# The first gate round in halves of 32 first keys, the second half among V blocks 0 to 31, with ScalarE making eight of 16 tokens' second-key one-hots

## What is computed

```python
q = (h @ w_q).reshape(b, s, 8, 2, 128)               # 8 heads, two half queries
scores = einsum('bshpd,hpnd->bshpn', q, sub_keys)    # 128 scores per half
top_s, top_i = top_k(scores, 16)                     # first keys and second keys
cand = top_s[..., 0, :, None] + top_s[..., 1, None, :]
best_s, best_pos = top_k(cand, 16)                   # expert = first key * 128 + second key
gates = softmax(best_s)
act = gelu(x . u_tab[expert])                        # 8 heads x 16 experts per token
out = sum(gates * act * v_tab[expert])
x = layer_norm(alpha * h + out)
```

## Time and profile before

| | |
|---|---|
| median of 3 executions | 1513.28 us (1513.22, 1513.28, 1518.79) |
| profiled execution, its own time | 1518.35 us |
| its span | 1516.2 us |
| busy share of the span | PE 89%, PEld 63%, DVE 77%, ACT 21%, POOL 44% |
| moved by DMA | 444.24 MB, mean 293 GB/s |
| longest rows of the chain that ended last | PE L1232 34%, DMA of `peer_v` rows 11%, PE L1249 7%, PE L1285 6% |

### The profile page before, as it was taken

The page is one execution under the profiler, slowest core; times in us unless marked ns, Lnnn a source line. Parts: engine busy times, 40 slices in busy tenths (PEclk is TensorE's granted clock), DMA queues, the critical chain, the costliest instruction groups (busy, mean ns, idle before and its releaser), DMA issues.

```text
span 1516.2 us, 18422 instructions
## 1 busy us (share of the span) xinstructions
PE 1354.7 (89%) x6418; PEld 953.7 (63%) x6418; DVE 1175.1 (77%) x2515; ACT 317.7 (21%) x609; POOL 660.3 (44%) x548
## 2 busy tenths in 40 slices
PE   8999989999999996764899799999799999999940
PEld 6787755688888885554444345588688874444410
DVE  5746345778888898779987799989888887666698
ACT  4223010111111011110010355556531110000010
POOL 2244111141443345600365465645365665656572
PEclk9999999999999997875899999999899999999975
DMA  6311422475888989920599999989799999999995
GB/s 230 144 57 56 152 74 96 138 225 174 328 336 342 357 303 401 407 109 1 187 413 415 413 373 364 406 337 391 259 380 383 414 414 412 414 413 415 412 358 215
DMA packets 118283, 444.24 MB, mean 293 GB/s; under 512 B 11568, under 2 KB 24368, under 8 KB 101808
## 3 DMA queue, kind: packets, MB, share of 16 engines
q0 software_dynamic: 73728, 268.47, 46.1%
q1 hardware_dynamic: 43888, 173.56, 29.6%
q10 hardware_dynamic: 576, 1.05, 0.2%
HBM read 440.93 MB, written 2.10 MB: 292 GB/s over the span
## 4 chain that ended last, share of the span: by engine, by line
PE 54%; DVE 17%; DMA 15%; issue 5%; POOL 5%; DVEq 3%; ACT 1%; ACTq 0%; SPq 0%
PE ps L1232 34%; DMA big<-in_peer_v_dram,idx 11%; PE ps L1249 7%; PE ps L1285 6%; DMA big<-in_peer_u_dram,idx 4%; DVE y L1071 3%; POOL big L566 3%; DVE big L1050 2%; POOL big L556 2%; PE ps L1457 2%; DVE pool_mem L1134 1%; DVE ohi L1091 1%; DVE wr L1090 1%; PE ps L1391 1%; PE ps L1372 1%
## 5 line engine op out<-in xcount | busy, mean ns | idle before, releaser
L556 POOL DMA_INDIRECT big<-in_peer_u_dram,idx x256 | 310.1, 1211 | 580.3 <-DVE dots L1050 463.5
L1071 DVE SCALAR_TENSOR_TENSOR y<-big,wgt,y 128x1024 f32<-128x1024 f32 x256 | 328.2, 1282 | 44.4 <-DMA big<-in_peer_v_dram,idx 32.3
L1050 DVE CUSTOM_DVE_ANT_0 big<-big,xh 128x1024 f32<-128x1024 f32 x256 | 311.5, 1223 | 63.1 <-DMA big<-in_peer_u_dram,idx 35.8
L566 POOL DMA_INDIRECT big<-in_peer_v_dram,idx x256 | 289.2, 1130 | 113.8 <-issue 70.2
L1232 PE MATMUL ps<-xT,big 128*128 128x256 f32 x1024 | 230.8, 384 | 11.7 <-issue 11.7
L1285 PE MATMUL ps<-big,pool_mem 128*128 128x512 f32 x512 | 226.1, 597 | 0.0
L1232 PEld LDWEIGHTS ps<-xT,big 128*128 128x128 f32 x1024 | 196.5, 193 | 40.8 <-issue 14.5
L1285 PEld LDWEIGHTS ps<-big,pool_mem 128*128 128x128 f32 x512 | 97.4, 192 | 119.7 <-issue 119.7
L1285 PE MATMUL ps<-y,pool_mem 128*128 128x512 f32 x256 | 116.5, 606 | 0.8 <-DVEq L1207 0.8
L1232 PE MATMUL ps<-xT 128*128 128x256 f32 x512 | 116.0, 386 | 0.0
L1232 PE MATMUL ps<-xT,y 128*128 128x256 f32 x512 | 114.7, 383 | 0.0
(11 more groups left out here) (224 smaller groups left out, 1445.9 us busy)
## 6 DMA issues: line engine op xcount, KB each, us to landing
big<-u_pairs_dram SPq DMA_DIRECT2D x32, 1024.0 KB
big<-v_pairs_dram SPq DMA_DIRECT2D x32, 1024.0 KB
y<-u_pairs_dram SPq DMA_DIRECT2D x16, 1024.0 KB
xT<-u_pairs_dram SPq DMA_DIRECT2D x16, 1024.0 KB
y<-v_pairs_dram SPq DMA_DIRECT2D x16, 1024.0 KB
xT<-v_pairs_dram SPq DMA_DIRECT2D x16, 1024.0 KB
big<-in_w_in_dram SPq DMA_DIRECT2D x24, 512.0 KB, 5.7
pool_mem<-in_peer_w_q_dram SPq DMA_DIRECT2D x12, 1024.0 KB
```

Of the source, the lines that this page charges most:

```text
L556: nc.gpsimd.indirect_dma_start(urow[n % RING], None, peer_u2, bass.IndirectOffsetOnAxis(ap=idx[:, u, e:e + 1], axis=0)).then_inc(s_u[n % R ...
L566: nc.gpsimd.indirect_dma_start(vrow[n % RING], None, peer_v2, bass.IndirectOffsetOnAxis(ap=idx[:, u, e:e + 1], axis=0)).then_inc(s_v[n % R ...
L1050: V.tensor_tensor_reduce(out=urow[n % RING], in0=urow[n % RING], in1=xh[:, u // PH * D:(u // PH + 1) * D], scale=1.0, scalar=0.0, op0=ALU. ...
L1071: V.scalar_tensor_tensor(acc_rows[t], vrow[n % RING], wgt[:, u % 2, e:e + 1], acc_rows[t], ALU.mult, ALU.add).then_inc(s_vadd, 1)
```

## The change

The gate round of 32 groups goes. In its place are 16 teams (0, 0, m) at row 80, of 16 tokens and first keys 0 to 31, and 16 teams (0, 1, m), of first keys 32 to 63, at rows 81 to 109 of DVE. For teams (0, 0, m) DVE makes both `ohj` matrices, in three buffers that take turns (`ohj3`: the two of `ohj` and the memory of `ohl`); for teams (0, 1, m) ACT makes the second one, as in round 1. PE has the teams (0, 1, m) ahead of `expert` 1, 2, 4, 6, 8, 9, 11, ..., 27 of round 0. `dense_weights` now covers 32 keys of 16 tokens; that of team (0, 1, m) follows the DVE work of team m + 2, the last two stand at row 110. `expert` 0 waits for the first 32 keys, `expert` 32 for the others. ACT's gelu of unit 5 moves from ahead of the round to behind team (0, 1, 8).

```diff
-SPREAD = ((1, 0), (1, 1))
+SPREAD = ((0, 1), (1, 0), (1, 1))
...
     def gate_round():
-        for n in range(GROUPS):
-            add("gate", n, by="dve")
+        for m in range(TEAMS):
+            add("team", 0, 0, m, by="dve")
...
         if r == 0:
-            jobs.append(("onehot", (0, 0), None))
+            jobs.append(("onehot", (0, 1, 0), None))
         for n in range(HALF):
+            if r == 0 and n < QUARTER:
+                for m in range(TEAMS):
+                    if n == 1 + m * 7 // 4:
+                        add("team", 0, 1, m, by="dve")
+                        jobs.append(("onehot", (0, 1, m + 1) if m + 1 < TEAMS else (1, 0, 0), None))
+                        if m == 8:
+                            jobs.append(("gelu", (5,), None))
...
-    dense_second_half(0, range(4, 6))
+    dense_second_half(0, range(4, 5))
...
                 if kind == "onehot":
-                    s, m = arg
+                    m = arg[2]
+                    b, n = BANK[TEAM[TEAM0[arg[0:2]] + m - 1]]
+                    act.wait_ge(full[b], n + 1)
...
-                V.tensor_tensor(ohj[:, g % 2], spread(1, 2 * m, NK), both(grid[:], NK), ALU.is_equal)
-                fence().then_inc(s_oh, 1)
+                if g >= TEAMS:
+                    V.tensor_tensor(ohj[:, g % 2], spread(1, 2 * m, NK), both(grid[:], NK), ALU.is_equal)
+                    fence().then_inc(s_oh, 1)
+                for side in range(2) if g < TEAMS else ():
+                    e = 2 * g + side
+                    if e >= 3 and e % 2:
+                        dve.wait_ge(s_ohd, (e - 3) // 2 + 1)
+                    elif e >= 3:
+                        b, used_ = BANK[TEAM[(e - 3) // 2]]
+                        dve.wait_ge(full[b], used_ + 1)
+                    V.tensor_tensor(ohj3[e % 3], spread(1, 2 * m + side, NK), both(grid[:], NK), ALU.is_equal)
+                    fence().then_inc(s_oh, 1)
...
-                x3 = X[:, :, 8 * n:8 * n + 8]
-                V.scalar_tensor_tensor(x3, ps[:, b, :].rearrange("p (t i) -> p i t", t=8), 1.0 / GATE_SCALE, x3,
+                x3 = X[:, QUARTER * s:QUARTER * (s + 1), 16 * m:16 * m + 16]
+                V.scalar_tensor_tensor(x3, ps[:, b, :].rearrange("p (t i) -> p i t", t=16), 1.0 / GATE_SCALE, x3,
                                        ALU.mult, ALU.mult).then_inc(free[b], 1)
...
-                    for g in range(GROUPS):
-                        gate_rows(g)
-                        if g:
-                            dense_weights(g - 1)
-                    dense_weights(GROUPS - 1)
+                    for m in range(TEAMS):
+                        team_rows_of(0, 0, m)
+                        if m:
+                            dense_weights(0, m - 1)
+                    dense_weights(0, TEAMS - 1)
                     fence().then_inc(s_wgtd, 1)
                 for r, s, m in teams_after(n):
                     team_rows_of(r, s, m)
+                    if r == 0 and m >= 2:
+                        dense_weights(1, m - 2)
+                if n == team_rows(0, 1)[-1] + 1:
+                    dense_weights(1, TEAMS - 2)
+                    dense_weights(1, TEAMS - 1)
+                    fence().then_inc(s_wgtd, 1)
...
-                    if i == 0 and r == 0:
-                        pe.wait_ge(s_wgtd, 1)
+                    if i % QUARTER == 0 and r == 0:
+                        pe.wait_ge(s_wgtd, i // QUARTER + 1)
...
-                elif kind == "gate":
-                    n_ = arg[0]
-                    pe.wait_ge(s_oh, n_ + 1)
...
+                        e = 2 * g + t // 8
+                        if g < TEAMS:
+                            hot = ohj3[e % 3]
...
+                        if t == 7 and g < TEAMS:
+                            last.then_inc(s_ohd, 1)
```

More of the change, by code:

```diff
@@ L22 @@
 ROWS = GUNITS * TOPK
-GROUPS = DENSE // 8
 LAG = 2 * TOPK
@@ L177, in dense_first_half @@
                 if n + 1 < TEAMS:
-                    jobs.append(("onehot", (1, n + 1), None))
+                    jobs.append(("onehot", (1, 1, n + 1), None))
             add("act", r, n, by="act" if r == 0 else "dve")
@@ L200, in dense_second_half @@
                 add("team", 1, 0, m, by="act")
-                jobs.append(("onehot", divmod(m + 1, TEAMS), None))
+                jobs.append(("onehot", (1,) + divmod(m + 1, TEAMS), None))
                 if m in between:
@@ L252, in layer @@
     BANK = {(kind,) + arg: (b, n) for kind, arg, _, b, n in JOBS}
-    TEAM = [("team",) + rs + (m,) for rs in SPREAD for m in range(TEAMS)]
-    TEAM0 = {rs: k * TEAMS for k, rs in enumerate(SPREAD)}
+    TEAM = [("team",) + rs + (m,) for rs in ((0, 0),) + SPREAD for m in range(TEAMS)]
+    TEAM0 = {rs: k * TEAMS for k, rs in enumerate(((0, 0),) + SPREAD)}
     ctx = ExitStack()
@@ L334, in layer @@
         ohj = wr[:, :].bitcast(f16).rearrange("p (b q n t) -> p b q n t", b=2, q=2, t=4)
+        ohj3 = [ohj[:, 0], ohj[:, 1]]
         lookd = wr[:, :].bitcast(bf16)
@@ L370, in layer @@
         sel = sb("sel", [P, 2, 2, PH, TOPK])
-        ohl = sel[:].rearrange("p a b h k -> p (a b h k)").bitcast(f16).rearrange("p (q n t) -> p q n t", q=2, t=4)
+        ohj3.append(sel[:].rearrange("p a b h k -> p (a b h k)").bitcast(f16).rearrange(
+            "p (q n t) -> p q n t", q=2, t=4))
+        ohl = ohj3[2]
         gated = sb("gated", [P, 2 * PH, TOPK])
@@ L416, in layer @@
         s_gates, s_selT = sem("gates_ready"), sem("selT_ready")
-        s_oh, s_ohl = sem("onehots_ready"), sem("last_eight_onehots_ready")
+        s_oh, s_ohd, s_ohl = sem("onehots_ready"), sem("first_onehots_used"), sem("last_eight_onehots_ready")
         s_act, s_wgtd = sem("dense_gelu_ready"), sem("dense_weights_ready")
@@ L1126, in gate_pieces, with dense_weights @@
                     fence()
-            def dense_weights(n):
-                b, used_ = BANK["gate", n]
+            def dense_weights(s, m):
+                b, used_ = BANK["team", 0, s, m]
                 dve.wait_ge(full[b], used_ + 1)
-                if n == 0:
+                if s == 0 and m == 0:
                     dve.wait_ge(s_act, 1)
-                x3 = X[:, :, 8 * n:8 * n + 8]
-                V.scalar_tensor_tensor(x3, ps[:, b, :].rearrange("p (t i) -> p i t", t=8), 1.0 / GATE_SCALE, x3,
+                x3 = X[:, QUARTER * s:QUARTER * (s + 1), 16 * m:16 * m + 16]
+                V.scalar_tensor_tensor(x3, ps[:, b, :].rearrange("p (t i) -> p i t", t=16), 1.0 / GATE_SCALE, x3,
                                        ALU.mult, ALU.mult).then_inc(free[b], 1)
@@ L1199, in _ @@
                     gate_pieces()
-                    first_key(0)
-                    fence()
-                    for g in range(GROUPS):
-                        gate_rows(g)
-                        if g:
-                            dense_weights(g - 1)
-                    dense_weights(GROUPS - 1)
+                    for m in range(TEAMS):
[3 more added lines that the diff above has]
+                    dense_weights(0, TEAMS - 1)
                     fence().then_inc(s_wgtd, 1)
@@ L1450, in _ @@
                     for t in range(16):
[L1451 to L1455, removed]
+                        e = 2 * g + t // 8
+                        if g < TEAMS:
+                            hot = ohj3[e % 3]
+                        else:
+                            hot = ohj[:, g % 2] if t < 8 else ohl
+                        if t % 8 == 0 and g < TEAMS:
+                            pe.wait_ge(s_oh, e + 1)
+                        elif t == 0:
+                            pe.wait_ge(s_oh, TEAMS + g + 1)
+                        elif t == 8:
+                            pe.wait_ge(s_ohl, g - TEAMS + 1)
                         for c in range(PIECES):
```

## The result

The changed kernel takes 1522.78 us in the median of 8 runs (1518.55 to 1524.15), the kernel before 1513.84 (8 runs, 1512.22 to 1518.79). The ratio is 1.0051, with an interval of 1.0037 to 1.0065: 7.7 us slower (5.6 to 9.8). The forecast was + 6.0 us. The profiled executions stand at 1523.54 and 1518.35 us, 5.2 apart.

The account below looks back on a forecast made before the run. DVE was taken to bound the gate round and, with the moved teams, rows 80 to 110. - 23.0 + 41.0 - 17.1 = + 1.0 us on DVE, + 5.0 through PE: + 6.0, 1519.3 us against the median, range 1511 to 1532.

Parts of the forecast that it names:

- The round: Gate round at row 80: 3.31 us per team, V block 0 at 706.5 against 729.46, 23.0 us earlier.
- + 41.0 us on DVE among rows 80 to 110: Sixteen moved teams (0, 1, m) between rows 81 and 109 add 16 x 2.56 = 41.0 us of DVE work.
- - 17.1 us of gather waits: Rows 80 to 110: the added work fills all 17.1 us that DVE waited for gathered rows.
- Rival 1: Rows 80 to 110: gathers keep DVE waiting; half the old waits gives + 14.5 us, 1527.8; chance 0.28.
- DVE's path to team (1, 0, 0): From V block 0 to row 111: 100.0 + 41.0 us, reaching 847.5 against 846.5, + 1.0 us.
- PE's path: V blocks 0 to 31: PE waits about 21 us for DVE, team (1, 0, 0) 13.8 us late; + 5.0 us through PE.
- The end: From team (1, 0, 3) on PE is 6.0 us late, as are (1, 1, 12) and all behind it, a rigid tail.
- Rival 4: Moved teams: ACT's one-hots come late and PE waits behind token 7; priced at nothing, no chance given.
- Rival 2: V blocks 0 to 31: PE's clock drops after waits, a loss of 2 to 5 us, + 8 to + 11; chance 0.14.
- Rival 3: Rows 80 to 110 bound by DMA, not DVE: row 111 at 823.5, up to - 23.0 us, 1490.3; chance 0.08.
- The rule weighed: Rows 80 to 110: two-SBUF-input DVE instructions shut out GpSimd, so 64 new ones would slow POOL's gathers; no size of its own.

Follow-up runs that it names:

- e3_dve_both: Changed kernel, but DVE, not ACT, makes the second-key one-hots of the moved teams (0, 1, m) too; ratio to the kernel before 1.0137.
- e4_all_in_round: DVE makes all one-hots and all 32 teams of round 0 stand in the round, none among rows or V blocks; ratio to the kernel before 1.0217.
- e6_before_act: The kernel before, but ACT makes the second-key one-hots of every third group, 11 of 32; 1497.16 us, ratio to the kernel before 0.9953.
- before_again: The kernel before unaltered, one execution for its trace on a third chip; 1513.41 us.
- e2_pe_later: Changed kernel, but PE's list has team (0, 1, m) ahead of V block 1 + 2m, DVE's list untouched; ratio to the kernel before 1.0016.
- after_third: The changed kernel unaltered, one execution on the third chip; 1527.71 us.
- after_again: The changed kernel unaltered, timed again on the chip of the experiments; 1512.42 us against 1504.93, ratio to the kernel before 1.0046.

## Why the prediction was right, point by point

- **The round.** Pitch 3.31 forecast, 663.75 - 660.42 = 3.33 in the trace. V block 0 at 705.21 against 706.5, of which 0.7 is the earlier start. Right.
- **+ 41.0 us on DVE among rows 80 to 110.** DVE takes 140.4 us from V block 0 to row 111 (845.65); less the 100.0 of the rows that is 40.4. The same term in the pair `e3_dve_both` and `e4_all_in_round`: 41.0 forecast, 13.0 more for the one-hots that DVE makes there, less 17.8 of gather waits, 36.2 us; row 111 moved by 35.0. The sizes agree within about 1 us.
- **- 17.1 us of gather waits.** They are gone whole: DVE waits for no gather before row 111, against a forecast of under 3 us. Rival 1 fell. Of the 17.1, name a gather for 13.4; the other 3.7 stand under "issue", with no releaser, and the prediction took them as gathers too. They are gone as well. The term came from one execution. The other three traces with an unfilled stretch have 17.1 (8.7 + 8.4 in `e6_before_act`), 17.8 (`e4_all_in_round`) and, with PE's pause in it, 13.5 (`before_again`), so it was sized near the usual value.
- **DVE's path to team (1, 0, 0).** 140.4 us against 141.0. Row 111 comes 0.9 us earlier than before; + 1.0 was forecast.
- **PE's path.** Team (0, 1, 15) 839.40 against 840.6; (1, 0, 0) 861.15 against 862.3; (1, 0, 3) 885.19 against 886.3; no wait at either. PE waited for DVE 15.8 us among blocks 0 to 27, not 21; 1.6 more for ACT; 4.0 more went into the two slower stretches behind its long waits (16 records from 725.79 on took 9.15 us and from 801.28 on 8.95, against 7.03). One wait was other than forecast: PE was to find team (0, 1, 15) not ready, but the last wait for DVE is 0.56 us at team (0, 1, 13), and DVE had team 15's one-hot ready at about 838.5, 0.9 us before PE came: from team 13 on PE's steps of 8.01 us were longer than DVE's of 7.6. DVE's stall at team (1, 0, 9) is 2.17 us, with 1.53 and 1.13 more around it (2.7 forecast, in one; DVE stood 1.9 us earlier than forecast). In the interval 23.3 of the 28.1 us are ahead of row 111 on DVE and 4.8 come through PE, forecast at 5.0. These are shown on their own: `e2_pe_later` takes that lateness away, and 6.1 us of the interval come back.
- **The end.** `gated_gelu` 0 at 995.59 (996.8), (1, 1, 12) at 1097.27 (1099.5). So team (1, 1, 12) was 3.8 us later than before where 6.0 were forecast, and the tail, forecast as rigid, was 1.6 us longer. That the span's + 5.4 lies so near + 6.0 is in part luck: the two misses nearly cancel. The runs' + 7.7 is 2.3 above the span's difference, and where that comes from was not found.
- **Rival 4.** ACT's one-hot was late once, 1.6 us at team (0, 1, 5). PE waited for DVE 6.05 us further on, so it cost nothing, as the prediction had priced it. In `after_third` it was late behind PE's last wait for DVE, and its 0.97 us did show.
- **Rival 2, PE's clock.** Its sign came, but not its price. Behind the wait of 6.05 us the granted clock is 0.50, inside V block 18, and the two blocks there lost 1.9 us; the mean of 0.97 over 729.4:846.5, the same as before, hides this. The loss was made good by team (0, 1, 13), where PE still waited 0.56 us for DVE. The rival had asked for 2 to 5 us. The margin was that thin: in `after_third` the step behind the wait lost 2.7, and at team (0, 1, 13) no wait for DVE was left. Windows as in the earlier trace rows:

```profile
801.30:804.00 2.70, 2.70 (x9) 1.15 (x6) 2.57 (x4) 2.52 (x8) 1.38 (x1) 0.50 0.69 225
...
810.00:815.00 5.00, 5.00 (x42) 2.85 (x41) 4.70 (x7) 3.61 (x9) 3.86 (x4) 1.00 0.96 362
```

- **Rival 3** fell with `e3_dve_both`, and row 111 came at 845.65, not at 823.5.

Two things stay open. The forecast of + 6.0 lies just inside the 7.6 us taken as no change, the measured + 7.7 just outside, and both intervals (here and in `after_again`, + 4.5 to + 9.3) hold both sides of that line. And the runs of one kernel stand in groups some 5 us apart (after: three near 1518.6, five at 1522.4 to 1524.2; before: 1512.2 to 1514.1, and 1516.0 to 1518.8). What makes the groups, and why the one pair on the third chip stands 14.3 us apart, was not found.

**The rule weighed.** POOL's gathers beside the rows, before (730:846) and after (705.2:845): busy us, mean ns | idle before them.

```profile
L556 POOL DMA_INDIRECT big<-in_peer_u_dram,idx x31 | 35.5, 1146 | 127.0 <-DVE dots L1050 118.9 <-issue 8.1
L566 POOL DMA_INDIRECT big<-in_peer_v_dram,idx x30 | 33.8, 1128 | 13.9 <-issue 8.2 <-DVE y L1071 5.6
...
L565 POOL DMA_INDIRECT big<-in_peer_u_dram,idx x31 | 42.2, 1360 | 128.3 <-DVE dots L1061 124.7 <-issue 3.7
L575 POOL DMA_INDIRECT big<-in_peer_v_dram,idx x30 | 29.8, 995 | 10.4 <-issue 8.5 <-DVE y L1082 1.9
```

The u gathers issued more slowly (1734 ns in the median of 31, against 937), the V gathers faster, and all 61 together took 72.0 us instead of 69.3. The slower ones agree with what the Trainium skill says in SBUF — State Buffer, Who interferes with whom: a DVE instruction with two SBUF inputs contends with a GpSimd instruction that reads SBUF. The faster ones do not speak for it, and no run here tells it from other causes of a slow issue. (Of the 64 new instructions that the prediction counts under the rule, the 16 products read PSUM and have one SBUF input; and the rival that prices late gathers is its first, not its second.) The slower issues cost nothing: DVE waited for none of these gathers. POOL's 124.7 us of idle ahead of them are its waits for DVE to free a buffer, 71.2 of them over the round.

## What to carry to other kernels

Work moved out of a stretch where one engine is the bound is free only up to that engine's waits in the stretch that takes it. Add up those waits first (here some 17 us), then what the split itself adds (here 18, second-key one-hots made twice and fences): that it could not pay is there before any detail. The rest of the loss, some 5 us, came from where PE's list had the moved work, and another order there gave 6.1 us of the interval back. Removing work from the bound engine, onto one that idles in the same stretch, kept all it saved: eleven of 32 one-hots on ACT, in the kernel left otherwise as it was, gave 7 us. When two engines hand buffers to each other in a written order, shift neither list alone without the other's pace in hand: with two buffers a lead of two teams is a stall.

## What had not been expected of the hardware

- PE can pause 1 to 2 us at a time ahead of single matmuls and wait for nothing that the trace shows. These pauses came in four of the twelve traces, at the same places of the program in the kernel before and the changed one (571 to 592 and 621 to 641), 22 us in `before` and in `after`, and in one trace once more among the V blocks. With them the changed kernel's round starts at 655.46 and 656.74, without them at 641.12.
- The interval of the changed kernel, in which work fills DVE's waits, was 392.1, 392.0 and 393.2 us in three executions; that of the kernel before was 364.0 and, with such a pause in it, 359.8.
- An indirect DMA's issue on POOL at nearly twice its time (937 to 1734 ns in the median) made no gather late.
- The last part, thought rigid, takes 422.7 to 425.9 us in kernels with the same instructions in it, without a pattern that these runs show.
